# A decoder block on one core: the first modulation and the first products of u in two halves of the model width

## What is computed

```python
mod = silu(c) @ w_ada + b_ada                 # 6 x 1024
sh1, sc1, g1, sh2, sc2, g2 = split(mod, 6)
h = rms_norm(x, norm1_g) * (1.0 + sc1) + sh1
proj = h @ w_in                               # q 512 | k 128 | v 128 | u 512
q, k = rope(rms_norm(q)), rope(rms_norm(k))   # angles = positions * inv_freq
attn = sliding_window_sink_attention(q, k, v) # window 128
pooled = causal means of u over 2, 4, 8, 16 tokens, minus u
x = x + g1 * (concat[attn, pooled @ pool_w * pool_scale] @ w_o)
x = x + g2 * (relu(h2 @ w1) ** 2 @ w2)        # h2 from x, sc2, sh2
```

## Time and profile before

| | |
|---|---|
| time, median of 3 runs | 937.52 us (936.0 to 938.73) |
| time of the profiled execution | 938.53 us |
| its span in the profile | 936.8 us |
| busy: VectorE, ScalarE, GpSimd | 650.0, 495.9, 361.0 us |
| mean granted TensorE clock | 0.998 of full speed |
| DMA | 175.54 MB, mean 187 GB/s |

### The profile page before, as it was taken

One profiled execution on the slowest core, in us unless ns is written; L12 is line 12 of the kernel. 1 busy time (PEld: TensorE's weight loads), 2 busy tenths in 40 slices (PEclk: granted clock), 3 DMA queues, 4 the chain that ended last, 5 costly groups with the idle time before them and its releaser, 6 DMA issues.

```text
span 936.8 us, 12630 instructions
## 1 busy us (share of the span) xinstructions
PE 914.9 (98%) x4399; PEld 766.6 (82%) x4399; DVE 650.0 (69%) x1001; ACT 495.9 (53%) x869; POOL 361.0 (39%) x347
## 2 busy tenths in 40 slices
PE   2999999999999999999999999999999999999998
PEld 2888888887888888888888888888888888888886
DVE  6978887888645778556554654445786666689896
ACT  2667888786655546554455544536334444333431
POOL 8162322243422446888888888721000000000000
PEclk9999999999999999999999999999999999999999
DMA  9953232235122423746555553359999638986773
GB/s 355 360 174 114 81 117 86 91 112 182 45 90 90 134 69 128 242 160 202 186 172 169 178 182 135 113 172 330 348 346 311 201 102 291 311 291 217 248 248 110
DMA packets 92271, 175.54 MB, mean 187 GB/s; under 512 B 9320, under 2 KB 26288, under 8 KB 92208
## 3 DMA queue, kind: packets, MB, share of 16 engines
q1 hardware_dynamic: 92096, 174.70, 55.4%
q10 hardware_dynamic: 112, 0.04, 0.0%
HBM read 136.95 MB, written 37.75 MB: 186 GB/s over the span
## 4 chain that ended last, share of the span: by engine, by line
PE 95%; DVE 2%; DMA 1%; ACT 1%; SPq 1%; issue 0%; POOL 0%; DVEq 0%; POOLq 0%
PE psum L2064 27%; PE psum L2062 27%; PE psum L2063 27%; PE psum L2058 4%; PE psum L2156 1%; PE psum L2157 1%; PE psum L2160 1%; PE psum L2142 1%; DMA xh<-in_x 1%; PE psum L2175 1%; DVE w_o_lo L1372 1%; PE psum L2202 1%; PE psum L2232 1%; PE psum L2075 1%; PE psum L2235 1%; PE psum L2238 1%
## 5 line engine op out<-in xcount | busy, mean ns | idle before, releaser
L1115 ACT CAST down_operands<-down_raw 128x1024 fp32r<-128x1024 f32 x96 | 101.1, 1055 | 152.8 <-PE psum L2064 63.6
L2062 PE MATMUL psum<-down_operands 128*128 128x512 f32 x448 | 174.3, 389 | 0.0
L2063 PE MATMUL psum<-down_operands 128*128 128x512 f32 x448 | 174.3, 389 | 0.0
L2064 PE MATMUL psum<-down_operands 128*128 128x512 f32 x448 | 174.3, 389 | 0.0
L1777 DVE TENSOR_TENSOR down_operands<-down_raw,down_operands 128x1024 fp32r<-128x1024 f32 x93 | 112.5, 1220 | 18.9 <-ACT down_operands L1115 18.3
L2062 PE MATMUL psum<-h2T,w_operands 128*128 128x512 f32 x272 | 106.0, 390 | 0.1
L2064 PE MATMUL psum<-h2T,w_operands 128*128 128x512 f32 x272 | 105.9, 389 | 0.0
L2063 PE MATMUL psum<-h2T,w_operands 128*128 128x512 f32 x272 | 105.8, 389 | 0.0
L2063 PEld LDWEIGHTS psum<-down_operands 128*128 128x128 f32 x448 | 84.1, 188 | 17.6
L2062 PEld LDWEIGHTS psum<-down_operands 128*128 128x128 f32 x448 | 84.1, 188 | 17.5
L2064 PEld LDWEIGHTS psum<-down_operands 128*128 128x128 f32 x448 | 84.1, 188 | 17.3
(11 more groups left out here) (285 smaller groups left out, 1962.3 us busy)
## 6 DMA issues: line engine op xcount, KB each, us to landing
down_raw<-in_w_mlp_out SPq DMA_DIRECT2D x160, 256.0 KB, 4.3
down_raw<-act_scratch SPq DMA_DIRECT2D x112, 256.0 KB, 3.3
raw<-in_w_ada SPq DMA_DIRECT2D x32, 512.0 KB, 4.6
raw<-in_w_mlp_in SPq DMA_DIRECT2D x32, 512.0 KB, 5.0
act_scratch<-act_quads_a SPq DMA_DIRECT2D x64, 256.0 KB, 2.2
act_scratch<-act_quads_b SPq DMA_DIRECT2D x48, 256.0 KB, 3.6
slots<-in_w_ada SPq DMA_DIRECT2D x8, 512.0 KB, 10.6
xh<-in_x SPq DMA_DIRECT2D x8, 512.0 KB, 5.8
```

The source lines that it names most:

```text
L1115: nc.scalar.copy(o[:, 0, :, :], r[:, 0:2, :]).then_inc(op2_hi, 1)
L2062: mm(o, wh, ah, start=first, stop=False, skip_group_check=adds)
L2063: mm(o, wh, al, start=False, stop=False, skip_group_check=adds)
L2064: return mm(o, wl, ah, start=False, stop=last, skip_group_check=adds)
```

## The change

The pieces of the first modulation are cut the other way: a piece "mod" holds 512 columns of the shift and the same 512 of the scale, in 2 KB rows. The first eight give the first half of the width for both, the last eight the second. Two pieces of u's weights stand between them, two behind. Tile 0 of x is loaded behind the third piece, tile 1 behind the second of u's weights.

With the first half of a1 and b1, ScalarE makes the first halves of h of tiles 0 and 1, one after the other, and TensorE the twelve products of each for u (`project_u_half`), in two PSUM banks. With the second half (`make_h_front` on VectorE for tile 0, ScalarE for tile 1) come the other twelve of each. Then q, k, v of tile 0 follow slice by slice, and behind them, without a u in between, the pooling windows and tile 2.

The angles move on VectorE to behind the first half of the sums (with inverse frequencies that GpSimd writes into a row, one operation in place of eight), the sines on ScalarE ahead of u's third weight piece. Tile 0 and tile 1 get a root each. GpSimd casts u's second weight piece. Tile 0's first window columns come from a small band of their own (`band_first`, four more products), so that GpSimd rewrites nothing. The second half of tile 2's h goes from VectorE to ScalarE. The parameters are loaded ahead of tile 2. There are more calls of `keep_clock`.

```diff
-        stream = [("sh1", k) for k in range(KD)]
-        stream += [("sc1", k) for k in range(KD)]
-        stream += [("wu", k) for k in range(KD // 2)]
+        stream = [("mod", k) for k in range(KD)]
+        stream += [("wu", 0), ("wu", 1)]
+        stream += [("mod", KD + k) for k in range(KD)]
+        stream += [("wu", 2), ("wu", 3)]
...
+        POOL_CASTS = ((1,), ())
+        HI_COUNT = ((1, 1, 2, 3), (1, 2, 3, 4, 5, 6, 7, 8))
...
-        def xT_banks(t):
-            return banks({0: 6, 1: 4, 2: 4}.get(t, 1))
+        def xT_block(t, k):
+            at = {0: (6, 7), 1: (4, 5), 2: (4, 5)}.get(t, (1, 2))[k // NK]
+            return bank(at)[:, (k % NK) * P:(k % NK + 1) * P]
...
+        def h_step(t, h):
+            return (1, 3, 2, 4)[2 * t + h] if t < 2 else 2 * t + h + 1
...
+        def front_summed(piece):
+            return piece + 1 + (piece >= KD) + (piece % KD == KD - 1)
...
+            if kind == "mod":
+                half = k // KD
+                return wada[:, k % KD, 0:2 * D].rearrange("p (m d) -> p m d", m=2)[:, :, 512 * half:512 * half + 512]
...
-                    sp.wait_ge(h_lo, 2 * (t - 1))
+                    sp.wait_ge(h_lo, h_step(t - 2, 1))
                 sp.dma_start(xh[:, t % 2, :], x_rows[t * P:(t + 1) * P, :]).then_inc(x_in[t % 2], 16)
             sp.dma_start(cin, c[0].rearrange("(p k) -> p k", k=KD)).then_inc(c_in, 16)
             first_job = place[("sh2", 0)]
             for n in range(first_job):
                 load(n)
-                if n == 7:
+                if n == 2:
                     load_x(0)
+                if n == place[("wu", 1)]:
                     load_x(1)
-            load_x(2)
             sp.dma_start(scale_row, pool_scale.to_broadcast([P, PW])).then_inc(params_in, 16)
...
+            load_x(2)
+            load_x(3)
             for t in range(NT):
-                if 1 <= t and t + 2 < NT:
+                if 2 <= t and t + 2 < NT:
...
-            def make_h_half(t):
-                if t == 0:
-                    act.wait_ge(a1_ready, 2)
+            def make_h_half(t, h):
+                if t < 2:
+                    act.wait_ge(a1_ready, h + 1)
+                    if h == 0:
+                        act.wait_ge(mod_taken, 1)
+                    else:
+                        act.wait_ge(b1_second, 1)
                 act.wait_ge(x_turned, t + 1)
-                for k in range(NK, KD):
-                    ins = nc.scalar.activation(xh[:, t % 2, k * P:(k + 1) * P], xT_banks(t)[:, k * P:(k + 1) * P],
+                for k in range(NK * h, NK * h + NK):
+                    ins = nc.scalar.activation(xh[:, t % 2, k * P:(k + 1) * P], xT_block(t, k),
                                                ACT.Identity, bias=b1[:, k:k + 1], scale=a1[:, k:k + 1])
-                ins.then_inc(h_half[1], 1)
+                ins.then_inc(h_half[h], 1)
...
+                    act.wait_ge(u_done, 1)
...
+            def hi_h_first():
+                for n, (made, done) in enumerate(((h_front, h_front_hi), (h_half[1], h_hi))):
+                    act.wait_ge(made, 1)
+                    nc.scalar.copy(hTh[:, 4 + 2 * n:6 + 2 * n, :], xh[:, 0, 512 + 256 * n:768 + 256 * n]
+                                   .rearrange("p (k n) -> p k n", n=P)).then_inc(done, 1)
...
+            square_x(0)
+            scale_x(0)
+            hi_wu(0)
+            make_h_half(0, 0)
+            hi_h(0, 0)
+            square_x(1)
+            scale_x(1)
+            make_h_half(1, 0)
+            hi_h(1, 0)
+            sines()
+            hi_wu(2)
+            hi_h_first()
+            hi_wu(3)
+            make_h_half(1, 1)
+            hi_h(1, 1)
+            for k in range(5):
+                hi_wqkv(k)
             keep_u(0)
-            hi_h(1, 0)
-            hi_h(1, 1)
+            for k in range(5, KD):
+                hi_wqkv(k)
+            keep_u(1)
             square_x(2)
             square_q(0)
             square_kv(0)
             hi_v(0)
             scale_x(2)
-            sines()
-            keep_u(1)
             keep_pooled(0)
+            make_h_half(2, 1)
             hi_h(2, 0)
             hi_h(2, 1)
...
+                own_d.step(v.tensor_tensor(a0.rearrange("p (t f) -> p t f", f=HALF), bcast(cols[:, 64:72], 2, HALF),
+                                           bcast(inv_row, 1, NT), ALU.mult))
...
+            def sum_front(half):
+                sums = acc_sc if half else acc
+                for k in range(KD):
+                    if k >= 1:
+                        dve.wait_ge(mod_summed, front_summed(KD * half + k - 1))
+                    if k < KD - 1:
+                        add_piece(sums[:, :], ("mod", KD * half + k), k, mod_summed)
+                    else:
+                        a = landed(dve, ("mod", KD * half + k))
+                        for m in range(2):
+                            cut = slice(512 * m, 512 * m + 512)
+                            v.scalar_tensor_tensor(out=sums[:, cut], in0=a[:, cut], scalar=silu[:, k:k + 1],
+                                                   in1=sums[:, cut], op0=ALU.mult, op1=ALU.add).then_inc(mod_summed, 1)
+                    if half == 0 and k == 1:
+                        dve.wait_ge(rows_in, 16 * 4)
+                        v.tensor_copy(rows[64:72, :], posi[64:72, :]).then_inc(posf_ready, 1)
+                    if half == 0 and k == 2:
+                        dve.wait_ge(rows_turned, 1)
+                        v.tensor_copy(cols[:, :], psum[:, 0, 0:72]).then_inc(cols_ready, 1)
+                    if half == 1 and k == 4:
+                        lo_h(1, 0)
...
+            def shift_1(h):
+                if h == 0:
                     dve.wait_ge(cols_ready, 1)
                     dve.wait_ge(mod_turned, 1)
-                    v.tensor_tensor(b1.rearrange("p (h k) -> p h k", h=2), psum[:, 0:2, 0:4],
-                                    cols[:, 8 * SH1:8 * SH1 + 8].rearrange("p (h k) -> p h k", h=2),
-                                    ALU.add).then_inc(mod_taken, 1)
+                    v.tensor_tensor(b1[:, 0:4], bank(1)[:, 0:4], cols[:, 8 * SH1:8 * SH1 + 4], ALU.add).then_inc(mod_taken, 1)
+                else:
+                    dve.wait_ge(sc1_turned, 2)
+                    v.tensor_tensor(b1[:, 4:8], bank(2)[:, 0:4], cols[:, 8 * SH1 + 4:8 * SH1 + 8],
+                                    ALU.add).then_inc(b1_second, 1)
...
+            def make_h_front():
+                dve.wait_ge(b1_second, 1)
+                dve.wait_ge(a1_ready, 2)
+                dve.wait_ge(x_turned, 1)
+                for n, done in enumerate((h_front, h_half[1])):
+                    for k in (NK + 2 * n, NK + 2 * n + 1):
+                        ins = v.tensor_scalar(xh[:, 0, k * P:(k + 1) * P], xT_block(0, k),
+                                              a1[:, k:k + 1], b1[:, k:k + 1], ALU.mult, ALU.add)
+                    ins.then_inc(done, 1)
...
+            sum_front(0)
+            angles()
+            shift_1(0)
             scale_1(0)
-            make_h(0, 0)
+            lo_wu(0)
+            lo_wu(1)
+            lo_h(0, 0)
+            sum_front(1)
+            shift_1(1)
             scale_1(1)
-            lo_wu(0)
-            lo_h(0, 0)
-            lo_wu(1)
+            make_h_front()
+            lo_wu(2)
             lo_h(0, 1)
-            lo_wu(2)
             lo_wu(3)
-            for k in range(KD - 1):
+            lo_h(1, 1)
+            for k in range(KD):
                 lo_wqkv(k)
-            make_h(1, 0)
-            lo_wqkv(KD - 1)
-            lo_h(1, 0)
-            lo_h(1, 1)
...
+            def band_all(i):
+                band_of(i, band[:, i, 0:P], 0)
+                band_of(i, band[:, i, P:BAND], P)
+                own_p.step(less_token(i, P))
+            def hi_wu_second():
+                a = landed(pool, ("wu", 1))
+                g.tensor_copy(wih[:, 2:4, QKV:IN], a.rearrange("p (k n) -> p k n", k=2)).then_inc(wu_hi[1], 1)
+            inv = np.float32(ROPE_THETA) ** (-np.arange(0, ROT_DIM, 2, dtype=np.float32) / np.float32(ROT_DIM))
+            for f in range(HALF):
+                ins = g.memset(inv_row[:, f:f + 1], float(inv[f]))
+            ins.then_inc(ident_made, 1)
             for i, w in enumerate(POOL_WINDOWS):
-                own_p.step(g.memset(band[:, i, 0:P], 1.0 / w))
+                own_p.step(g.memset(band[:, i, :], 1.0 / w))
+            for s in range(MAX_WINDOW):
+                own_p.step(g.memset(band_first[:, s:s + 1], float(np.float32(1.0) / np.float32(s + 1))))
             own_p.wait()
-            for i, w in enumerate(POOL_WINDOWS):
-                if i == NP - 1:
-                    pool.wait_ge(x_squared, 2)
-                    root(rx[:, 0:2], ssx[:, 0:2], D, x_root)
...
+            own_p.step(g.affine_select(out=band_first, in_=band_first, compare_op=ALU.is_ge, fill=0.0, base=0,
+                                       pattern=[[1, MAX_WINDOW]], channel_multiplier=-1))
```

(86 more changed lines are left out.)

233 lines of the change are left out of this document (74 added, 159 removed).

## The result

The changed kernel takes **947.0 us** in the median of six executions (943.25 to 947.66), the kernel before beside it 937.5 (936.0 to 939.1): the ratio is 1.0100, interval 1.0085 to 1.0115, so 9.5 us slower. Both kernels have executions with and without a stretch of TensorE at its low level, and the mean granted clock of an execution tells which. After: 943.25 at 1.000 (one of six), 946.8 to 947.7 at 0.995 or 0.996 (five of six). The profiled execution of after is the one at 1.000 (span 941.5), that of before was of the 0.998 kind.

What follows compares the result with a forecast made beforehand. TensorE, busy 98%, bounds the kernel; what moves is when its products begin. Products 9.0 later, then 15.1 instead of 21.1, 0.8 for clock, 1.2 at tile 2's turning: +5.0 on 937.52, so 942.5; range 936.6 to 948.

Steps and rivals of the forecast that it cites:

- rival (c): TensorE stays at the low clock through column sums and both new halves of u: +4 to +6 more, 947 to 949; chance 0.14.
- Step 1: VectorE's first half of the sums: last piece lands at 16.3, sums take 1.42, done at 17.7.
- Step 2: Angles on VectorE between the halves: 2.9 less 0.5, free at 20.1, covered by the column sums if those come in time.
- step 4: Up to VectorE's last sum: VectorE, not the transfers, sets the second half; 39.1 against 29.0 before.
- Step 3: First half's column sums: GpSimd's twelfth operation at 13.5, tile 0's root 16.3, ready at 24.0; VectorE idles 4 us.
- rival (a): Comes out tight: GpSimd's root by 13, column sums hidden behind the angles; -0.4 in total, up to +2.8; chance 0.30.
- Step 5: From the last sum through column sums and handover to TensorE's next product: 42.2 against 33.20 before, 9.0 later.
- Step 6: TensorE's remaining u products and slices: 15.1 instead of 21.1, plus 0.8 for low clock; ends 58.1, 3.8 later.
- Step 7: Turning of tile 2 waits for ScalarE's scaling behind the squares of q and k: 1.2 later, total +5.0.
- I cost these at nothing: ScalarE's half of tile 2, params and x loads on SP's queue, and GpSimd's dropped band rewriting were priced at nothing.
- The rule against the row: Skill: only much longer idle stretches lose TensorE's clock, sum 4.2; profile row: short waits can; prediction kept 5.0.
- (b): A real gain: VectorE keeps up with the transfers, last sum 32.8, products at 35.9, -3.3 in all; chance 0.06.

Runs made afterwards that it cites:

- experiment 1: The changed kernel again with no edit, for its clock: 946.6 us, ratio 1.0101.
- experiment 7: On top of experiment 2, angles and sines back in their old places: 941.3 us, ratio 1.0046.
- experiment 6: experiment 5 without the eight products of the identity between tile 0's first half of u and the turning of tile 1: 942.0 us, ratio 1.0048.
- experiment 5: On top of experiment 2, ScalarE squares tile 1 of x ahead of making tile 0's first half of h: 942.9 us, ratio 1.0062.
- experiment 10: On top of experiment 2, no narrow products in tile 0's pooling windows, and tile 2's scaling ahead of the squares of q and k: 942.3 us.
- experiment 2: The changed kernel with GpSimd's root of tile 3 back ahead of the root of tile 1's q and k: 943.6 us, ratio 1.0066.
- experiment 3: The changed kernel with twenty fillings in TensorE's wait ahead of the second pool_out, its cause left in: 944.6 us, ratio 1.0080.
- experiment 4: The kernel before with more fillings, keep_clock(10, 0) for keep_clock(4, 0), ahead of its first product of u: 936.5 us, ratio 0.9997.
- experiments 9: On top of experiment 2, u's fourth weight cast ahead of tile 0's second half of h, and ten more fillings before u's second half: 941.5 us.
- experiment 11: The changed kernel with the edits of experiments 2, 5, 6, 7, u's fourth weight cast earlier, and fillings moved from before to behind the second column sums: 938.7 us.
- experiment 12: experiment 4, made on the kernel before, with ten fewer fillings ahead of its column sums: 936.3 us, ratio 0.9995.

## Why the prediction was right or wrong

The sign was right, and 947.0 lies inside the range, 1 us from its end. The forecast of +5.0 was too small: +9.5 is outside the +2.8 to +8 of its own case, so that the time lies in the range is luck in part; its upper end stood there for rival (c). Two of the three things that were to refute the forecast happened: the root of tile 0 came by 13, and TensorE loses time behind the turning of tile 2.

Where the number went wrong shows when executions that both lose clock are compared, experiment 1's trace with that of before. The turning of tile 2 starts at 60.87 against 55.26, +5.6 where the prediction had +5.0. The second pooled product, behind the wait, starts at 81.12 against 73.62, +7.5, and the end is +9.2 (946.0 against 936.8). Up to the turning the sum was nearly right, by steps whose errors offset; what was missing lies behind it.

**Step 1** (first half at 17.7): 18.2. **Step 2** (angles 2.4, covered by the column sums): 3.1, and covered but for 0.8 (experiment 7). The 0.7 more is the one operation of L1269 held up beside GpSimd's cast of u's second weight piece; step 4 had put that cast at nothing and had not asked what it does to VectorE.

**Step 3 failed.** "I take 13.5" for GpSimd's twelfth operation and 16.3 for the root; they ended at 10.7 and 11.6. The lock-step was priced right: 1.28 beside a sum, 0.29 beside none. But the first operation started at 4.45 for 5.2, seven of the twelve were done by 6.97, and the early sums start up to 2.3 us apart (8.83, 11.14 on VectorE) and take 1.28 each, so that GpSimd went through in the pauses. Turning, fillings and all column sums of the first half took 5.0 (14.80 to 19.84) for 4.7: TensorE was at the high level there, and VectorE did not idle. (The step read 3.57 for the column sums of before as the low level by the ratio of the durations alone; the windows by time give 1.00 for that stretch.) That is rival (a)'s mechanism, and yet not its time. By (a) the last sum would end at 34.5 (39.1 - 3.9 - 0.7) and the next product come at 37.6; they came at 36.5 and 41.05.

**Step 4** held in its form: VectorE and tile 1's chain (square, root, scaling, turning, first half of h) set the last sum, not the transfers (in experiment 6 the chain is 1.7 earlier and the last sum 1.3). High part of tile 0 to high part of tile 1: 8.0 for 7.6. It ends at 36.5 for 39.1, all of it from step 3. What the step did not see is that the sixteen fillings in TensorE's list stand in that chain: 0.4 us in after, 3 us once ScalarE is early (experiment 5).

**Step 5** (42.2) came to 41.05, but by two errors that offset: the last sum 2.6 earlier, and column sums and handover 4.5 for 3.1, since the fillings of L2136 stood ahead of all sixteen.

**Step 6** (15.1 us to the end of the slices): 15.26 at the full clock. The 0.8 for the clock was too small: 3.4 in experiment 1's execution. The place was right, where TensorE comes out of the waits; the size was half of what before lost, 1.7 behind one short wait, and this kernel has two.

**Step 7** (+1.2): +1.1, partly for another reason. The windows alone would let the turning start at about 58.15 (the last pair at 57.83 and the 0.32 that such a pair takes), the scaling ends at 58.35, and it starts at 58.41. So the narrow products cost 0.9 where the step had 0.2, and the scaling adds the last 0.26. And half of the 1.1 is not to be had (experiment 10).

**"I cost these at nothing" failed** for GpSimd's order. The diff moves the root of tile 3 behind that of q and k, and the prediction looked there only for what was removed. It cost TensorE a wait of 1.95 us (1.8 of time) and, in the execution of experiment 1, 3.4 us of low clock behind it, 1.7 more; in the medians the wait and its clock are 3.0 (experiment 2).

**The rule against the row.** The traces speak for the row: with waits of 0.6 to 2 us left open, TensorE dropped to 1.2 GHz behind them in many executions, and with a wait filled fewer lost clock (experiment 3: three of six, where the changed kernel had nine of ten; experiment 4: none of eleven, where the kernel before had 20 of 45; experiments 9 and 11: none of sixteen). The wait alone does not decide, though: experiment 12 has it filled and lost clock in three of eleven with ten fewer fillings ahead of it, and experiment 7 has its waits open and lost none in four. The sum of 4.2 by the rule that a clock is only taken back over much longer idle stretches was the worse one. Of that page of the Trainium skill (TensorE: Matmul & The Clock Gate), the passage on psum-queue depth-cycling, where a TensorE that idles briefly between groups makes the clock oscillate, fits these traces better.

**The rivals.** (b) was refuted: no version comes near a gain. (c) named 947 to 949 and the clock, and got the time; but the low level lay at 41 to 48 (the second halves of u, which it had named) and at 82 to 85, not in the first column sums or the first halves, and explains only 2.3 of the 9.5 (3.75 that after's median is above its full clock, less 1.4 for before). The other 7.2 are there at the full clock: the later start of the products, the windows and the wait of the account above.

## What to carry to other kernels

Instructions that only fill an engine's time are items of its in-order list: when work is moved so that the engine becomes the late one, read them as costs first. When a diff reorders two short operations on a side engine, follow the later one to its last reader with its measured duration; here a root of 0.56 us, 4.2 us late, was three handovers away from TensorE and cost it 1.8. And compare two versions at one point of the trace behind which they are alike, in executions of one clock: here the account came out within 0.2 us, and for experiment 11 within 0.1.

## What the runs showed of the hardware

Waits of 0.6 us with little TensorE work around them were followed by 3.4 us at the low level in some executions of one and the same program and not in others: 20 of the 45 executions of the kernel before beside the experiments were at 0.998. With such a wait filled none of eleven was, at no gain in the median (936.5 against 936.3); with ten fewer fillings ahead of it three of eleven were. The granted clock of the windows does not show all: for 24.3 to 29.7 us of before and 23.9 to 28.4 of experiment 4 it is 1.00, and there 38 equal fillings took 5.60 and 4.68 us.

Eight fp32 matmuls of 2 to 16 columns, set between the wide ones, took the pooling windows from 0.97 to about 1.84 us (56.31 to 58.15), an estimate of 0.87 / 8 = 0.11 each.

GpSimd and VectorE hold each other up in both directions: a 128x128 select of GpSimd took 1.28 us beside a sum of VectorE and 0.29 beside none, and a 128x64 operation of VectorE 1.02 us beside GpSimd's cast and 0.22 otherwise. How much GpSimd gets done beside a row of sums hangs on the pauses between them: here twelve operations in 6.3 us.
